# Expert weights used as float32 in 32-column tiles, 96 token slots, seven raw weight slots

## The reference

```python
logits = xt.astype(f32) @ router.astype(f32)
top_val, top_exp = lax.top_k(logits, TOP_K)          # TOP_K = 2 of N_EXPERTS = 8
gates = jax.nn.softmax(top_val, axis=-1)
# the tokens of an expert e are gathered into blocks, and each block goes through
swiglu(xb, w_gate[e], w_up[e], w_down[e])            # (silu(x @ w_gate) * (x @ w_up)) @ w_down
# w_gate, w_up: 1024 x 3584, w_down: 3584 x 1024, float32, per expert
# y[token] += block_output * gate, then the residual and a final RMSNorm
```

## Time and profile before

| | |
|---|---|
| median of 3 runs | 1764.69 us (1764.63 to 1765.04) |
| the profiled execution | 1765.69 us, span 1763.8 us |
| TensorE busy | 1644.0 us (93%), weight loads 1379.3 us (78%) |
| VectorE busy | 1275.7 us (72%) |
| ScalarE busy | 966.9 us (55%) |
| moved | 423.5 MB, mean 240 GB/s |
| TensorE's clock | 0.961 of full speed over the span |

### The profile page before, as it was taken

How to read it: one execution, slowest core, us unless ns; L and a number is a source line. 1 busy time by engine, 2 the same in 40 slices (tenths; PEclk the granted TensorE clock), 3 DMA queues, 4 the chain that set the end, 5 groups by cost and what they waited for, 6 DMA issues and landing times.

```text
span 1763.8 us, 24430 instructions
## 1 busy us (share of the span) xinstructions
PE 1644.0 (93%) x9843; PEld 1379.3 (78%) x9843; DVE 1275.7 (72%) x1260; ACT 966.9 (55%) x848; POOL 140.5 (8%) x149
## 2 busy tenths in 40 slices
PE   6986799999994789899999999999999999999996
PEld 5854589999883678788888888788788788788885
DVE  5659444444638663488888798888898888888884
ACT  2225434334434222377677677676777677676773
POOL 2968000000000120000000000000000000000000
PEclk9998899999995889799999999999999999999999
DMA  9000355546330003379899899899899999998992
GB/s 301 2 1 1 133 201 192 191 142 217 112 122 1 2 3 112 140 257 375 326 359 374 313 370 371 306 376 374 308 369 332 355 372 329 355 373 331 349 375 85
DMA packets 189975, 423.52 MB, mean 240 GB/s; under 512 B 15114, under 2 KB 18260, under 8 KB 189780
## 3 DMA queue, kind: packets, MB, share of 16 engines
q1 hardware_dynamic: 187984, 420.91, 65.7%
q10 hardware_dynamic: 1924, 1.64, 0.3%
HBM read 421.49 MB, written 1.05 MB: 240 GB/s over the span
## 4 chain that ended last, share of the span: by engine, by line
PE 85%; DVE 10%; ACT 2%; issue 1%; DMA 1%; DVEq 0%; SPq 0%; ACTq 0%
PE bank L1737 22%; PE bank L1739 22%; PE bank L1738 22%; PE bank L1726 3%; PE bank L1582 2%; PE bank L2072 2%; PE bank L2079 2%; PE bank L2140 1%; PE bank L1619 1%; PE bank L1634 1%; PE bank L1695 1%; DMA ring<-in_moe_w_gate 1%; PE bank L1569 1%; PE bank L1543 1%; DVE xnT L950 1%
## 5 line engine op out<-in xcount | busy, mean ns | idle before, releaser
L1374 DVE TENSOR_TENSOR ring_r<-ring,ring_r 128x2048 fp32r<-128x2048 f32 x332 | 753.5, 2289 | 129.1 <-ACT ring_r L852 128.9
L852 ACT ACTIVATE ring_r<-ring 128x2048 fp32r<-128x2048 f32 x332 | 636.9, 1920 | 200.8 <-PE bank L1739 180.5
L1737 PE MATMUL bank<-ring_r 128*128 128x512 f32 x1344 | 537.3, 400 | 2.9 <-DVE ring_r L1457 2.6
L1739 PE MATMUL bank<-ring_r 128*128 128x512 f32 x1344 | 525.2, 391 | 0.0
L1738 PE MATMUL bank<-ring_r 128*128 128x512 f32 x1344 | 524.3, 390 | 0.0
L1737 PEld LDWEIGHTS bank<-ring_r 128*128 128x128 f32 x1344 | 252.8, 188 | 63.9 <-DVE ring_r L1374 6.9
L1738 PEld LDWEIGHTS bank<-ring_r 128*128 128x128 f32 x1344 | 252.9, 188 | 53.9 <-issue 3.3
L1739 PEld LDWEIGHTS bank<-ring_r 128*128 128x128 f32 x1344 | 252.6, 188 | 54.2
L1739 PE MATMUL bank<-arena_r,ring_r 128*128 128x256 f32 x688 | 193.4, 281 | 0.0
L1125 DVE TENSOR_TENSOR ring_r<-ring,ring_r 128x2048 fp32r<-128x2048 f32 (+1 forms) x46 | 98.9, 2153 | 123.1 <-ACT ring_r L689 122.9
L689 ACT ACTIVATE ring_r<-ring 128x2048 fp32r<-128x2048 f32 (+1 forms) x46 | 82.9, 1804 | 126.7 <-PE bank L1739 112.4
(11 more groups left out here) (388 smaller groups left out, 1719.3 us busy)
## 6 DMA issues: line engine op xcount, KB each, us to landing
ring<-in_moe_w_gate SPq DMA_DIRECT2D x56, 2048.0 KB, 8.0
ring<-in_moe_w_up SPq DMA_DIRECT2D x55, 2048.0 KB, 8.8
ring<-in_moe_w_down SPq DMA_DIRECT2D x55, 2048.0 KB, 8.1
ring<-in_ffn_w_gate SPq DMA_DIRECT2D x5, 2048.0 KB, 7.9
ring<-in_ffn_w_up SPq DMA_DIRECT2D x5, 2048.0 KB, 7.8
ring<-in_ffn_w_down SPq DMA_DIRECT2D x5, 2048.0 KB, 7.7
ring<-in_o_w_in SPq DMA_DIRECT2D x5, 2048.0 KB, 7.7
ring<-in_e_w_in SPq DMA_DIRECT2D x4, 2048.0 KB, 14.3
```

What stands on the lines that cost most here:

```text
L852: act_.activation(pair(NH0 + h)[0], halves[h % 2], ACT.Copy).then_inc(sem("hi_done"), 1)
L1374: v.tensor_tensor(lo, expert_place(h // 2, type(it) is int)[0][h % 2], hi.bitcast(f32), SUB).then_inc(sem("lo_done"), 1)
L1737: pe_.matmul(dst, w[0], x[0], start=start, stop=False, skip_group_check=True)
L1739: return pe_.matmul(dst, w[0], x[1], start=False, stop=stop, skip_group_check=True)
```

## The change

The expert weights are no longer split. They are used as float32, straight from their slots, and `CAP` becomes 96. The 96 slots are the columns of three tiles of 32 (`QUAD`). In `by_tokens` tile m multiplies the first 384 columns of the weights (`FM` = 384) with 32 tokens, and writes them to partitions 32m to 32m+31 of a bank. The fourth tile takes the other 128 columns, for the three groups of tokens one after the other, and writes them to partitions 96 to 127. So a bank holds 384 columns of use, silu and multiplication work on 128x384, H is turned with three transposes (`turn_hidden`), and `hidden` finds the pieces. Y is put together by ScalarE (its main part) and VectorE (six copies of 32x128, `y_side`). All seven slots hold raw expert blocks; `xg` and `ht` move to the buffer `yT`. SP waits for `block_used`, which TensorE raises at a block's end. An expert may now need up to three items, so the routing has three more small instructions. `keep_warm_tiles` goes, and the plain filler stands behind every norm.

```diff
-CAP = 128
+CAP = 96
+FM = FB - P
+QUAD = [slice(32 * i, 32 * i + 32) for i in range(4)]
...
-    EXPERT_SLOTS = [5, 3, 4]
+    EXPERT_SLOTS = [5, 0, 1, 2, 6, 3, 4]
...
         def load_expert(it, e):
             for j in range(NEB):
 
-                sp.wait_ge(sem("lo_done"), NHE * it + NH0 + 2 * j - 4)
+                sp.wait_ge(sem("block_used"), NEB * it + j - SLOTS + 1)
                 load_block(e, j)
...
-        def expert_hi(it, h):
-
-            halves, loaded, count = expert_place(h // 2, type(it) is int)
-            act.wait_ge(loaded, 16 * (NEB // 3) * it + 16 * count)
-            act.wait_ge(sem("pair_used"), NHE * it + NH0 + h - 2)
-            act_.activation(pair(NH0 + h)[0], halves[h % 2], ACT.Copy).then_inc(sem("hi_done"), 1)
...
-        def expert_lo(it, h):
-
-            dve.wait_ge(sem("hi_done"), NHE * it + NH0 + h + 1)
-            hi, lo = pair(NH0 + h)
-            v.tensor_tensor(lo, expert_place(h // 2, type(it) is int)[0][h % 2], hi.bitcast(f32), SUB).then_inc(
-                sem("lo_done"), 1)
...
+        for n in range(2, -(-T // CAP)):
+            link(v.scalar_tensor_tensor(cnt[:, 1, :], cnt[:, 0, :], n * CAP + 0.5, cnt[:, 1, :], ALU.is_gt, ADD))
...
-        link(v.tensor_scalar(MO["off"], MO["oh"], float(CAP), None, MUL))
+        off = MO["off"].rearrange("p (i e) -> p i e", e=NE)
+        link(v.tensor_tensor(off, item, cnt[:, 3, :][:, None, :].to_broadcast(sh3), SUB))
+        link(v.tensor_scalar(off, off, 1.0, float(CAP), ADD, MUL))
+        link(v.tensor_tensor(off, off, oh, MUL))
...
+        def y_side(n):
+
+            dve.wait_ge(sem("block_used"), NEB * n)
+            for i in range(2):
+                for m in range(3):
+                    last = v.tensor_copy(MO["Y"][QUAD[m], FB * i + FM:FB * i + FB],
+                                         bank[4 + i][QUAD[3], P * m:P * m + P])
+            last.then_inc(sem("Y_side"), 1)
...
-            if n in (1, 2):
-                keep_warm_tiles(spare)
-            else:
-                keep_warm(spare, WARM["norm_out"][n])
+            keep_warm(spare, WARM["norm_out"][n])
...
+        def by_tokens(b, x, w, start, stop):
+
+            for m in range(3):
+                pe_.matmul(b[QUAD[m], 0:FM], x(m), w[:, 0:FM], start=start, stop=stop, skip_group_check=True)
+            for m in range(3):
+                last = pe_.matmul(b[QUAD[3], P * m:P * m + P], x(m), w[:, FM:FB], start=start and m == 0, stop=stop,
+                                  skip_group_check=True)
+            return last
...
+                pe.wait_ge(loaded, count)
+                if kind == "down":
+                    for k in range(4):
+                        for i in range(2):
+                            last = by_tokens(bank[4 + i], lambda m: hidden(c, k, m), w[:, k, FB * i:FB * i + FB],
+                                             c == 0 and k == 0, c == NFC - 1 and k == 3)
+                else:
+                    for k in range(KD):
+                        last = by_tokens(bank[0 if kind == "gate" else 1], lambda m: xg[:, k, QUAD[m]], w[:, k, :],
+                                         k == 0, k == KD - 1)
+                last.then_inc(sem("block_used"), 1)
```

More of the change, by code:

```diff
@@ L910, in _ @@
-        act.sem_inc(sem("Y_copied"), 1)
+            if not peeled:
+                y_main(it)
+            for j, (kind, c) in enumerate(expert_steps):
+                if kind == "gate":
+                    act.wait_ge(sem("block_used"), NEB * it + j + 1)
+                    if c or not peeled:
+                        act.wait_ge(sem("H_done"), NFC * it + c)
+                    act_.activation(MO["silu"], bank[0][:, 0:FM], ACT.Silu).then_inc(sem("moe_silu"), 1)
+                    if c:
+                        ht_copy(it, c - 1)
@@ L914, in _ @@
             run_item(it)
-        act.wait_ge(sem("pair_used"), NHE * n_items + NH0)
-        for i in range(2):
-            last = act_.activation(MO["Y"][:, 512 * i:512 * i + 512], bank[4 + i][:, :], ACT.Copy)
-        last.then_inc(sem("Y_copied"), 1)
+        y_main(n_items)
         act.wait_ge(sem("acc_final"), 1)
@@ L1453, in onehots @@
             last.then_inc(sem("onehot_ready"), 1)
-        def gather_lo():
-            for i in range(2):
-                last = v.tensor_tensor(flat(xg[1][:, 4 * i:4 * i + 4, :]), bank[6 + i][:, :],
-                                       flat(xg[0][:, 4 * i:4 * i + 4, :]).bitcast(f32), SUB)
-            last.then_inc(sem("xg_lo"), 1)
         def add_scattered(t):
@@ L2078, in scatter @@
             for i in range(2):
-                last = pe_.matmul(bank[6 + i][:, :], MO["gatedT"][:, t * P:t * P + P],
-                                  MO["Y"][:, 512 * i:512 * i + 512], start=True, stop=True)
+                last = pe_.matmul(bank[6 + i][:, :], MO["gatedT"][0:CAP, t * P:t * P + P],
+                                  MO["Y"][0:CAP, FB * i:FB * i + FB], start=True, stop=True)
             last.then_inc(sem("scatter_done"), 1)
@@ new lines, in by_tokens, with hidden @@
+        def by_tokens(b, x, w, start, stop):
[5 more added lines that the diff above has]
+            return last
+        def hidden(c, k, m):
+            return ht[:, c % 2, k, QUAD[m]] if k < 3 else ht[:, c % 2, m, QUAD[3]]
@@ new lines, in turn_hidden @@
+        def turn_hidden(it, c):
+            pe.wait_ge(sem("H_done"), NFC * it + c + 1)
+            if c == NFC - 1:
+                pe.wait_ge(sem("ht_copied"), NFC * it + c)
+            for j in range(3):
+                last = pe_.transpose(bank[2][:, j * P:j * P + P], MO["H"][:, j * P:j * P + P], ident)
+            last.then_inc(sem("HT_done"), 1)
+        def run_item(it, peeled=False):
+            for j, (kind, c) in enumerate(expert_steps):
+                w, loaded, count = expert_place(it, j)
+                w = w.rearrange("p (k n) -> p k n", n=D if kind == "down" else FB)
+                if kind == "gate":
+                    if c == 0:
+                        pe.wait_ge(sem("xg_copied"), it + 1)
+                    if c or not peeled:
+                        pe.wait_ge(sem("moe_silu"), NFC * it + c)
+                if kind == "up" and (c or not peeled):
+                    pe.wait_ge(sem("H_done"), NFC * it + c)
+                if kind == "down":
+                    pe.wait_ge(sem("ht_copied"), NFC * it + c + 1)
+                pe.wait_ge(loaded, count)
+                if kind == "down":
+                    for k in range(4):
+                        for i in range(2):
+                            last = by_tokens(bank[4 + i], lambda m: hidden(c, k, m), w[:, k, FB * i:FB * i + FB],
[5 more added lines that the diff above has]
+                last.then_inc(sem("block_used"), 1)
@@ L2131, in run_item @@
                     for t in range(NT):
-                        last = pe_.transpose(bank[3][:, t * P:t * P + P], gated[:, t, :], ident)
+                        last = pe_.transpose(bank[3][0:CAP, t * P:t * P + P], gated[:, t, :], ident)
                     last.then_inc(sem("gatedT_done"), 1)
-                if (kind == "gate" and c) or (kind == "up" and c == NFC - 1):
-                    cc = c if kind == "gate" else NFC
-                    pe.wait_ge(sem("H_done"), NFC * it + NFC + cc)
-                    if cc == NFC:
-                        pe.wait_ge(sem("ht_lo"), NFC * it + cc - 1)
-                    for j in range(4):
-                        last = pe_.transpose(bank[2][:, j * CAP:j * CAP + CAP], MO["H"][:, j * P:j * P + P], ident)
-                    last.then_inc(sem("HT_done"), 1)
+                    turn_hidden(it, c)
+                if kind == "gate" and c:
+                    turn_hidden(it, c - 1)
         pe.sem_inc(sem("scatter_done"), NT)
```

207 lines of the change are left out of this document (61 added, 146 removed).

## The result

The changed kernel takes 1779.78 us (median of 4 runs, 1778.65 to 1781.8), the kernel before 1764.66 (4 runs): a ratio of 1.0088, 95% interval 1.0071 to 1.0106. It is slower by 15 us, where 1758 was forecast. The profiled execution has a span of 1776.8 us against 1763.8.

A forecast was written before the change was run, and what follows sets the result against it. TensorE was taken as the bound, transfers a close second. Terms -33.8 + 9.2 + 2.6 + 4.5 - 3.5 + 14.7 - 0.2 = -6.5 us on 1765.69 gave 1759.2; the median, 1.0 lower, gave 1758, range 1741 to 1786.

The forecast's parts named there:

- (5): Turn of TensorE's loop over items: a code fetch at each jump back, 2.4 us, +2.1 over today's, seven times, +14.7.
- the turn of the loop is dear: Rival at the loop's turn: 4.0 us of standing plus 1.6 of lower clock, seven times, +22, 1780; chance 0.23.
- step 3: Weight split removed in each block: half of the 1.05 us left open returns, -0.5 in seven items, -3.5.
- the argument "against": At the loop's turn, against a dear turn: TensorE's queue holds work for some of the wait; no size given.
- (1): Products of the expert blocks: 0.3275 us a pass, 336 passes an item, 4.2 us less each; eight items, -33.8 us.
- The drift: Rival in the products: the column tiles drift, 0.340 us a pass over 2688 passes, +33.6, 1792; chance 0.09.
- tiles don't slow one another: Denies a rival in the products: tiles sharing one bank take 0.43 us a pass, +276 us, 2034; chance 0.02.
- (2): Array shape changes around full-array steps, 0.32 us there and back: turned tiles +9.2, gathers +2.6, scatters +4.5.
- (4): Seven raw weight slots in place of three: SP runs six blocks ahead, transfers at 389 GB/s keep ahead; counted 0.
- (6): Kernel's ends: subtractions -1.3, routing about +1.0, Y copies +0.3, 0.2 gained behind the first norm; sum -0.2.
- the gap between the last down block and the first gate block: Sign at the loop's turn: TensorE stands there in items 2 to 8, with some 17 instruction packets in every item.
- Gathers over 125.7 apart: Sign of being wrong, in the expert stage: gathers were forecast about 125.1 us apart, against 125.65 before.

The follow-up runs named there:

- e3: Kernel before with two items in one pass of TensorE's loop and item 1 written out: 1766.92 us, ratio 1.0017.
- e5: Changed kernel, SP holding one load of each further item back by one block so no weight transfer is in flight at the jump: 1761.63 us, ratio 0.9981.
- e10: Changed kernel with the jump named ahead and the fourth tile's pieces left out: 1720.84 us in one run.
- e8: Changed kernel with the jump named ahead and each scatter product as four 32-column matmuls on four tiles: 1735.56 us, ratio 0.9839.
- e6: Changed kernel with the jump named ahead and SP only three blocks ahead of TensorE instead of seven: 1744.68 us, ratio 0.9894.
- e4: Changed kernel with most products left out, which shortens TensorE's loop body to some 1560 instructions: 1625.3 us, one time.
- e9: Changed kernel with the jump named ahead, scatters on four tiles, and four and three filler calls behind the last block: 1735.96 us, ratio 0.9841.
- e7: Changed kernel with the jump named ahead and nine and five filler calls on TensorE behind the last block: 1737.38 us, ratio 0.9847.
- e12: Changed kernel with the jump named ahead, scatters on four tiles inside the loop, full array behind it, no filler: 1734.92 us, ratio 0.9833.
- e2: Changed kernel with TensorE's seven further items written out, the loop kept for items above eight alone: 1734.54 us, ratio 0.9836.

## Why the prediction was wrong

The step that failed is (5), the turn of the loop. It took 2.4 us, seven times; it is 7.08, six times. That is 42.5 in place of 16.8, +25.7 us, and turns the forecast of -6.5 into a loss. The prediction's rival "the turn of the loop is dear" named the place and the mechanism and gave 1780, which is the time that came, at a chance of 0.23; its terms were off and offset one another (4.0 of standing and 1.6 of clock, against 4.85 and 2.17; seven turns, against six). That the number fits to the microsecond is luck: its turns come to 39.2 us where 42.5 were lost, and the rest of the sum was wrong by more in the other direction (step 3).

What was wrong in the 2.4: I priced the fetch by a small transfer in an idle stage, the router's 32 KB. The fetch itself takes 3.4 to 3.8 us from the jump with the engines free (e3, e5), and 5.7 to 6.1 with a weight block in flight, behind which its packet starts. In this stage the engines are in use 93% of the time, and the jump comes 3.7 us after an issue in every item, not at random. Then I left the clock out of the likeliest case; a stand of 2.6 to 2.8 us brought the lower level in four of six in e5's profiled execution. That TensorE's queue covers some of it was the argument "against"; it is 1.2 us here, and 2.7 in the kernel before with the longer body (e3), where each queued record stands for four times as long (2 in 0.2267 us against 12 in 0.3275).

The other steps, by their own numbers:

(1) The products: right. Passes are 0.3275 us apart, by the fourth tile's pieces, and wide tiles alone give 0.3225 (e10). The drift that a rival feared is 0.005 us a pass and ends with each block; tiles don't slow one another.

(2) The change of shape: right. TensorE around a turned tile and a scatter (answers to the earlier trace rows):

```profile
1255.87 1.98 PE L2008 MATMUL bank<-arena 96*128 96x512 f32 x4
1257.78 0.52 PE L2019 MATMUL bank<-ring,yT 128*32 128x384 f32 x3
...
1263.16 0.55 PE L2035 MATMUL bank<-con,arena 128*128 128x128 f32 x3
1263.64 0.52 PE L2019 MATMUL bank<-ring,yT 128*32 128x384 f32 x3
```

A block of 16 passes takes 5.24 us of products and 5.38 from such a step to the next, 0.14 more (0.04 in its first pass, 0.10 behind its last); the turned tile has 0.48 more, 0.62 in all (0.65 forecast); a scatter 1.91 + 0.14 against 1.72, 0.33 (0.32 forecast). e8 takes the changes away from the scatters and gets 0.62 an item back for two.

(3) The split's late halves: undersized. 336 passes (110.04), six turned tiles (3.72), two scatters (4.10) and the stretch from gather to the seventh turned tile (4.43) are 122.29, the whole item. Nothing is left over, so all of the 1.05 us of before went, not half. Without the turns the stage is 29.4 us shorter, where 23.1 were forecast (21.0, and the 0.3 of today's turn seven times); 1.6 of the difference are the eight slow products at the start of the stage, which the changed kernel's execution does not have.

(4) Seven slots at no cost: right, and TensorE waits for none. It would not have been right for fewer: a lead of three blocks gives 9 us away (e6). The ceiling of 389 GB/s was sound (394 in e4).

(6) The ends: -0.2 forecast, 0.0 measured, but as a sum of two misses. The head gained 3.3: 1.4 at the first product (1.3 forecast for the subtractions), and 1.9 ahead of the gather, in stages where the two executions differ in when the clock falls; that part isn't traced to the change. The tail lost 3.3: the copies of Y take 1.93 us against 1.22, since six small ones follow one another on VectorE, and the scatters 2.81 and 3.80 against 1.99 and 2.00, at the lower clock:

```profile
1754.59 1.83 DVE L1428 COPY arena<-bank 32x128 f32<-32x128 f32 x6 [14.35 <-PE bank L2021]
1756.52 2.80 PE L2008 MATMUL bank<-arena 96*128 96x512 f32 x4 [1.97 <-issue]
1760.70 3.78 PE L2008 MATMUL bank<-arena 96*128 96x512 f32 x4 [1.38 <-DVE arena L1415]
```

Of what would show it, the gap between the last down block and the first gate block came, and packets in every item: 97 between 1000 and 1700 us, 18 an item (17 forecast). "Gathers over 125.7 apart" was the sign of being wrong, and they are.

Together: the turns +25.7, the rest of the stage -6.3 (29.4 against 23.1), the ends +0.2, which is 19.6; from -6.5 forecast to 13.0 measured between the profiled executions it is 19.5. The other 2 us are the step from that execution to the median, which lies 1.1 us above it and not 1.0 below.

What stays open: how far the wait for a weight block grows when several are queued ahead of the code packet; no run had that at a jump. Why the tail's clock falls in some executions and not in others was not tried further, nor why the code behind the loop comes late in e8 and e9 and in time in e7. What the turned tiles' changes of shape would give back was not run.

## What to carry to other kernels

Count the instructions of a loop's body on each engine before a change multiplies them: work cut into column tiles costs no TensorE time here, but 3.6 times the instructions (4160 records an item against 1151), and a body that is no longer kept pays at every jump back. Name the jump ahead, or write the items out; it cost one argument and gave 44 us. When a stall is a fetch, look at what else is queued on the same engines at that moment, and at what the clock does behind it.

## What the runs showed of the hardware

- The code packet of a jump waits for a weight transfer that is in flight: it starts 3.2 to 3.6 us after the jump behind one of 2 MB, about 1.0 us with none (12 jumps of the changed kernel and e5, no exception). Where the transfer was issued at the jump itself (e3), it started after 1.0 as well.
- The end of the loop is a place of its own. With the jump back named, TensorE stood behind the loop after 13 pairs of instructions, 2.1 to 3.6 us from start to start, while a packet came in that had started 4.4 us after the last branch (e8, e9). It did not with 8 pairs (e12), nor with 36, where the packet started after 1.4 us (e7). That the naming is the reason was not tried apart.
- Matmuls on four column tiles with 12 records in 0.3275 us, 37 a microsecond, ran for 120 us with nothing lost to the handing out of instructions, while each was fetched anew (e2).
